# Spreading a gain vector over the partitions with four matmuls instead of a broadcast load, at the head of a hybrid layer

## The chip, the cores and the metric

The kernel runs on one core of one Trainium2 chip. The metric is the device time of one execution in microseconds (us), as the median of several runs; less is better. The engines are named as the profile names them: PE is TensorE (PEld its weight loads), DVE VectorE, ACT ScalarE, POOL GpSimd, SP SyncE, which here only issues transfers (SPq in the rows).

## The reference, cut to what matters

The kernel computes one layer of an encoder for 512 prompt tokens and 64 sample tokens, in fp32, with a width of 2048. Everything starts from a normalised copy of the input:

```python
def rmsnorm(x, g):
    xf = x.astype(jnp.float32)
    xf = xf * lax.rsqrt(jnp.mean(xf * xf, axis=-1, keepdims=True) + RMS_EPS)
    return (xf * g.astype(jnp.float32)).astype(x.dtype)
...
    xn = rmsnorm(x, g_pre)

    def cols(off, width):
        return jnp.einsum('btd,dc->btc', xn, w_in[:, off:off + width])
```

The columns of `w_in` feed three token mixers (pooling, stick-breaking attention, mLSTM) with their gates; their outputs are projected by `w_branch`, merged, projected by `w_out`, normalised and added to x. `g_pre` has 2048 elements, one for each channel, and is the same for every token.

## The kernel before, in words

**Layout and blocks.** Tokens come in five blocks: four of 128 prompt tokens and one of 64 sample tokens. Block m of the input lies in `xt[:, m, :]` with tokens on partitions and the 2048 channels along each partition. So `g_pre`, which varies along the channels, is needed on all 128 partitions: `gpre_b` is a 128x2048 tile.

**The head of the program.** For each block ACT squares and sums the row (`square`, L1150), DVE makes the mean (`mean_square`, L1540), ACT takes the root (`root`, L1155), DVE takes the reciprocal (L1546) and multiplies x by it and by the gain in one instruction (`normalise`, L1549). PE then transposes the block in 16 pieces of 128x128, four to a PSUM bank (`x_block`, L772), and the banks go to `xq`, the even ones by ACT (L1162) and the odd ones by DVE (`x_quads`, L1557). Blocks 0 and 2 to 4 use the PSUM tensor `M`, block 1 uses `pp`. When blocks 0 to 2 are there, the first half of `xq` is split into a high and a low part by ACT (L1169) and DVE (L1566), and PE starts the products (L764) of w_in, also split into `wa_hi` and `wa_lo` (L1137 and L1526).

**The products.** Pairs of column tiles are computed by a Strassen scheme of seven products of 128x288 with quarters of x and w, or sums of them. The sums of x are made once, by DVE (L1570), while the first products run. There are 68 pairs, then the attention and mLSTM heads woven with the branch projections (L916), the output projection (L1099) and the last normalisation.

**What sets the order.** Each engine's program is written out by hand, and semaphores join them. An engine runs its instructions in that order, and what waits holds up all that stands behind it. On DVE the order is: a memset, the casts of `negones` and `negtri` (L1535, L1536), the mean and `normalise` of block 0, those of block 1, the copies of block 0, the mean and `normalise` of block 2, and so on. On ACT: square 0, root 0, square 1, root 1, two copies of block 0, square 2, root 2, two copies of block 1. POOL starts four small loads and then makes the constants `ident`, `ones`, `negones_f` and `negtri_f`, each of which adds one to `consts_ready`. SP issues the loads in the order block 0, `gpre_b`, blocks 1 and 2, half a tile of w_in, block 3, and so on; the load of `gpre_b` reads the vector 128 times, once for each partition.

Of the kernel before, what the change touches and what calls it, by code (L numbers as in the profile page):

```python
# [10 lines left out]
P = 128  # L11
D = 2048
# [163 lines left out]
def hybrid_layer(nc, x_prompt, x_sample, cache_sb_k, cache_sb_v, state_pool, state_ml_c, state_ml_n,  # L176
# [30 lines left out]
    with ctx:  # L207
        start = -(-nc.sbuf_base // 32) * 32

        def sb(name, at, shape, dt=F32):  # L210
            return nc.alloc_sbuf_tensor_at(name, shape, dt, offset=start + at)

        def sem(name):
            return ctx.enter_context(nc.semaphore(name))
# [9 lines left out]
        ones = sb("ones", 41472, [P, P])  # L224
# [5 lines left out]
        R = 43264  # L230
# [24 lines left out]
        gpre_b = sb("gpre_b", R + 110592, [P, D])  # L255
# [2 lines left out]
        negones_f = sb("negones_f", R + 126976, [P, P])  # L258
        negtri_f = sb("negtri_f", R + 127488, [P, P])
        xq = sb("xq", R + 129024, [P, 4, HK, TH])  # L260

        if_w = [sb("if_w0", R + 150784, [P, HK, P]), sb("if_w1", R + 158080, [P, HK, P])]
        if_rows = sb("if_rows", R + 155648, [ROWS, T])
# [82 lines left out]
        def x_bank(m, q):  # L346

            return pp[:, q, :] if m == 1 else M[:, 512 * q:512 * (q + 1)]
# [46 lines left out]


        x_loaded = [sem(f"x_loaded{m}") for m in range(NB)]
        gain_loaded, vectors_loaded, consts_ready = sem("gain_loaded"), sem("vectors_loaded"), sem("consts_ready")
        signs_ready = sem("signs_ready")
        sq_done, ms_ready, root_x_ready, if_loaded = sem("sq_done"), sem("ms_ready"), sem("root_x_ready"), sem("if_loaded")  # L400
        xs_ready, xtr_done, xqa_done, xqd_done = sem("xs_ready"), sem("xtr_done"), sem("xqa_done"), sem("xqd_done")
# [55 lines left out]
        def _(sp):  # L457
# [15 lines left out]
            def x_block(m):  # L473
                if m < NT:
                    sp.dma_start(xt[:, m, :], xp_v[:, m, :]).then_inc(x_loaded[m], 16)
                else:
                    sp.dma_start(xt[0:TS, NT, :], x_sample[0, :, :]).then_inc(x_loaded[NT], 16)
# [5 lines left out]
            def gate_weights():  # L483

                sp.wait_ge(g_stored, 32 * PG)
                for j in range(2):
                    sp.dma_start(if_w[j][:, :, :], w_in_v[:, HK * j:HK * (j + 1), OFF_MI:OFF_MI + P]).then_inc(if_loaded, 16)

            x_block(0)
            sp.dma_start(gpre_b[:, :], g_pre[0, :].partition_broadcast(P)).then_inc(gain_loaded, 16)  # L490
            x_block(1)
            x_block(2)
            sp.dma_start(raw_11(At(0)), w_in_v[:, 0:HK, column_of(0):column_of(0) + P]).then_inc(wa_loaded[0], 16)
# [259 lines left out]
        def _(pe):  # L753
# [23 lines left out]
            def x_block(m):  # L777

                rows = P if m < NT else TS
                pe.wait_ge(xs_ready, m + 1)  # L780
                for q in range(4):
                    if m == 2:
                        pe.wait_ge((xqa_done, xqd_done)[q % 2], q // 2 + 1)
                    elif m == 3:
                        pe.wait_ge((xqa_done, xqd_done)[q % 2], 4 + q // 2 + 1)
                    elif m == 4:
                        pe.wait_ge(xqa_done, 6 + q + 1)
                    transposes([(x_bank(m, q)[:, P * j:P * j + rows],
                                 xt[0:rows, m, (4 * q + j) * P:(4 * q + j + 1) * P]) for j in range(4)]
                               ).then_inc(xtr_done, 1)  # L790

            pe.wait_ge(consts_ready, 4)
            x_block(0)
            x_block(1)
            x_block(2)
# [724 lines left out]
        def _(dve):  # L1520
            steps = Steps(dve, dve_steps)
# [9 lines left out]

            nc.vector.memset(small[:, 0:20], 1.0).then_inc(signs_ready, 1)
            dve.sem_inc(urow_copied, 1)
            dve.wait_ge(consts_ready, 4)
            nc.vector.tensor_copy(negones[:, :], negones_f[:, :]).then_inc(signs_ready, 1)  # L1535
            nc.vector.tensor_copy(negtri[:, :], negtri_f[:, :]).then_inc(signs_ready, 1)  # L1536
# [6 lines left out]
            def normalise(m):  # L1543
                rows = P if m < NT else TS
                dve.wait_ge(root_x_ready, m + 1)
                steps.link(nc.vector.reciprocal(rs_x[:, m:m + 1], rs_x[:, m:m + 1]))  # L1546
                if m == 0:
                    dve.wait_ge(gain_loaded, 16)
                nc.vector.scalar_tensor_tensor(xt[0:rows, m, :], xt[0:rows, m, :], rs_x[0:rows, m:m + 1],  # L1549
                                               gpre_b[0:rows, :], ALU.mult, ALU.mult).then_inc(xs_ready, 1)  # L1550

# [20 lines left out]
            steps.begin(0, NB)  # L1572
            mean_square(0)
            normalise(0)
            mean_square(1)
            normalise(1)
            x_quads(0)
            mean_square(2)
            normalise(2)
            x_quads(1)  # L1580
            x_quads(2)
# [809 lines left out]
```

## Time and profile before

| | before |
|---|---|
| median of 3 runs | 2336.64 us (2335.86 to 2339.87) |
| the profiled execution | 2337.64 us, of which its span 2334.4 us |
| PE busy | 2264.0 us, 97% of the span |
| DVE busy | 1463.8 us, 63% |
| ACT busy | 924.3 us, 40% |
| mean granted PE clock | 0.99 of full |

The span runs from the first to the last instruction of the trace; 3.2 us of the profiled execution lie around it. A row of the timeline has the start in us from the beginning of the span, the duration in us, then engine, line, operation, tiles and shapes; in square brackets stands the idle time ahead of it and what ended that. The page gives groups of instructions with their summed busy time and the mean of one in ns.

### The profile page before, as it was taken

To read this page: it belongs to the slowest core of one execution; us is meant where nothing else is said; L and a number is where in the kernel's file an instruction comes from. 1 tells how busy PE (TensorE), PEld (TensorE's weight loads), DVE (VectorE), ACT (ScalarE), POOL (GpSimd) and SP (SyncE) were. 2 spreads that over 40 slices of the span, in tenths; PEclk is the share of its full clock that TensorE was granted. 3 is DMA by queue.
4 is the path that set the end of the run, shared out by engine and by line. 5 is a ranking of instruction groups with operands and counts; after the bars stand their busy time and mean duration, and the time that the engine had idled before them with its cause. 6 is when DMAs were issued, how large, how long until landed. Compare 5 with 4: busy or idle time off the path is not lost.

```text
span 2334.4 us, 40379 instructions
## 1 busy us (share of the span) xinstructions
PE 2264.0 (97%) x16616; PEld 2226.1 (95%) x16616; DVE 1463.8 (63%) x1641; ACT 924.3 (40%) x1243; POOL 216.6 (9%) x288
## 2 busy tenths in 40 slices
PE   6899999899999999999999999999999999999996
PEld 5899999899999999999999999999898999999996
DVE  7866768556666666667666666664665676653233
ACT  5433433334433344444444444444554333222221
POOL 0000000000100000111000000000343222000000
PEclk9999999999999999999999999999999999999998
DMA  5443434433444444444444444347556556735222
GB/s 154 115 136 92 135 102 126 140 94 109 127 129 115 127 116 117 129 117 125 119 114 129 121 122 122 110 129 234 169 191 209 178 184 188 183 112 187 74 72 98
DMA packets 417517, 312.34 MB, mean 134 GB/s; under 512 B 11213, under 2 KB 378949, under 8 KB 415376
## 3 DMA queue, kind: packets, MB, share of 16 engines
q1 hardware_dynamic: 398512, 248.81, 38.5%
q0 software_dynamic: 18848, 61.25, 7.4%
q8 instruction: 122, 2.00, 0.4%
q14 instruction: 35, 0.29, 0.0%
HBM read 251.11 MB, written 58.90 MB: 133 GB/s over the span
## 4 chain that ended last, share of the span: by engine, by line
PE 89%; DVE 5%; DMA 2%; issue 1%; ACT 1%; POOL 1%; DVEq 0%; SPq 0%; POOLq 0%; ACTq 0%
PE pp L764 64%; PE pp L916 10%; PE pp L1099 8%; PE M L772 1%; PE M L973 1%; PE M L1019 1%; DMA raw_b<-in_w_out_dram 1%; PE M L1036 1%; PE M L953 1%; PE M L875 1%; PE M L943 1%; PE M L764 1%; DMA out_dram<-n_out 1%; DVE xa L1566 0%; PE M L1076 0%
## 5 line engine op out<-in xcount | busy, mean ns | idle before, releaser
L764 PE MATMUL pp<-xa,wa_hi 128*128 128x288 f32 x7584 | 1524.0, 297 | 18.6 <-DVE xa L1566 11.3
L764 PEld LDWEIGHTS pp<-xa,wa_hi 128*128 128x128 f32 x7584 | 1220.3, 188 | 20.6 <-issue 11.2
L764 PE MATMUL pp<-xa,wa_lo 128*128 128x288 f32 x3792 | 1118.8, 295 | 0.0
L764 PEld LDWEIGHTS pp<-xa,wa_lo 128*128 128x128 f32 x3792 | 717.3, 189 | 0.0
L1526 DVE TENSOR_TENSOR wa_lo<-raw_a,wa_hi 128x1024 fp32r<-128x1024 f32 x272 | 338.5, 1247 | 248.2 <-ACT wa_hi L1137 248.1
L1137 ACT ACTIVATE wa_hi<-raw_a 128x1024 fp32r<-128x1024 f32 x272 | 287.2, 1056 | 217.0 <-PE pp L764 204.4
L1526 DVE TENSOR_TENSOR wa_lo<-raw_r,wa_hi 128x1024 fp32r<-128x1024 f32 x134 | 170.8, 1275 | 142.5 <-ACT wa_hi L1137 142.5
L1137 ACT ACTIVATE wa_hi<-raw_r 128x1024 fp32r<-128x1024 f32 x134 | 141.5, 1056 | 132.3 <-PE pp L764 130.2
L916 PE MATMUL pp<-gt_hi,wb_hi 128*128 128x288 f32 x768 | 169.5, 302 | 0.5 <-DVE gz L1883 0.5
L916 PE MATMUL pp<-gt_hi,wb_lo 128*128 128x288 f32 x768 | 164.8, 296 | 0.0
L916 PE MATMUL pp<-gt_lo,wb_hi 128*128 128x288 f32 x768 | 164.6, 296 | 0.0
L2239 POOL DMA_DIRECT2D z_scratch<-zs x60 | 44.0, 733 | 1071.6 <-ACT zs L1285 581.4
L1526 DVE TENSOR_TENSOR wa_lo<-tx_main,wa_hi 128x1024 fp32r<-128x1024 f32 x67 | 82.1, 1226 | 69.5 <-ACT wa_hi L1137 69.5
L916 PEld LDWEIGHTS pp<-gt_hi,wb_hi 128*128 128x128 f32 x768 | 123.6, 190 | 1.1 <-DVE wb_lo L1871 0.7
L1530 DVE TENSOR_TENSOR raw_a<-raw_a 128x1024 f32<-128x1024 f32 x102 | 124.3, 1219 | 0.0
L916 PEld LDWEIGHTS pp<-gt_hi,wb_lo 128*128 128x128 f32 x768 | 123.9, 189 | 0.0
L916 PEld LDWEIGHTS pp<-gt_lo,wb_hi 128*128 128x128 f32 x768 | 123.7, 189 | 0.0
L1871 DVE TENSOR_TENSOR wb_lo<-raw_b,wb_hi 128x1024 fp32r<-128x1024 f32 x80 | 98.3, 1243 | 29.6 <-ACT wb_hi L1372 29.5
L1099 PE MATMUL pp<-m_hi,wb_hi 128*128 128x288 f32 x512 | 111.2, 298 | 1.3 <-DVE wb_lo L1871 1.3
L1372 ACT ACTIVATE wb_hi<-raw_b 128x1024 fp32r<-128x1024 f32 x80 | 83.8, 1052 | 69.1 <-PE pp L1099 30.9
L1099 PE MATMUL pp<-m_hi,wb_lo 128*128 128x288 f32 x512 | 109.9, 296 | 0.0
L1099 PE MATMUL pp<-m_lo,wb_hi 128*128 128x288 f32 x512 | 109.9, 296 | 0.0
(294 smaller groups left out, 2165.8 us busy)
## 6 DMA issues: line engine op xcount, KB each, us to landing
raw_a<-in_w_in_dram SPq DMA_DIRECT2D x204, 512.0 KB, 5.0
raw_r<-in_w_in_dram SPq DMA_DIRECT2D x68, 512.0 KB, 5.0
z_scratch<-zs POOLq DMA_DIRECT2D x60, 576.0 KB, 3.3
raw_b<-in_w_branch_dram SPq DMA_DIRECT2D x48, 512.0 KB, 4.3
raw_b<-in_w_out_dram SPq DMA_DIRECT2D x32, 512.0 KB, 4.4
gz<-z_scratch SPq DMA_DIRECT2D x48, 288.0 KB, 4.4
qkv<-z_scratch SPq DMA_DIRECT2D x23, 288.0 KB, 4.8
gt_hi<-gated_scratch SPq DMA_DIRECT2D x4, 1152.0 KB, 7.3
```

Of the source, the lines that this page charges most:

```text
L764: i = nc.tensor.matmul(out, ws[:, slot, k, :], xa[:, o, part, k, :], start=opens and k == 0 and s == 0, stop=k == HK - 1 and s == 2, skip_ ...
L772: i = nc.tensor.transpose(out, src, ident[0:k, 0:k])
L875: i = nc.tensor.matmul(out, wp[:, k, c * P:(c + 1) * P], pa[:, k, a:a + w], start=k == 0, stop=k == 1)
L916: i = nc.tensor.matmul(out[:, b, :], ws[:, slot, k, :], xs_[:, k, b * TH:(b + 1) * TH], start=k == 0 and q == 0, stop=k == HK - 1 and q == 2)
L943: m = nc.tensor.matmul(M[:, col:col + w], keys, qT[:, q0:q0 + w], start=True, stop=True)
L1099: i = nc.tensor.matmul(out[:, b, :], ws[:, slot, k, :], xs_[:, k0 + k, b * TH:(b + 1) * TH], start=opens and k == 0 and q == 0, stop=close ...
L1137: nc.scalar.activation(wa_hi[:, n.base % RING_A, :, :], src, ACT.Copy).then_inc(wa_hi_ready, 1)
L1372: nc.scalar.activation(wb_hi[:, n.base % RING_B, :, :], raw_b[:, n.base % RAW_B, :, :], ACT.Copy).then_inc(wb_hi_ready, 1)
L1526: nc.vector.tensor_tensor(wa_lo[:, n.base % RING_A, :, :], src, wa_hi[:, n.base % RING_A, :, :].bitcast(F32), ALU.subtract).then_inc(wa_lo ...
L1530: nc.vector.tensor_tensor(out, a, b, ALU.subtract).then_inc(t_ready, 1)
L1871: nc.vector.tensor_tensor(wb_lo[:, n.base % RING_B, :, :], raw_b[:, n.base % RAW_B, :, :], wb_hi[:, n.base % RING_B, :, :].bitcast(F32), A ...
L2239: pool.dma_start(z_v[:, bass.ds(p.times(2).value(-16), 2), :] if p.per else z_v[:, 2 * spill_of(p.base):2 * spill_of(p.base) + 2, :], stag ...
```

## The change

The vector is loaded first of all, as a single row of 8 KB on one partition (`gpre_row`). Four matmuls, each with a contraction over one partition, multiply a column of ones into 512 elements of the row and so leave each element on all 128 partitions of a bank of `M`. DVE copies the four banks to `gpre_b`, ahead of the two casts, and waits for the last copy. The broadcast load of 1 MB and the wait for it in `normalise` are gone. The loads of x blocks 0, 1 and 2 now follow one another.

```diff
+        gpre_row = sb("gpre_row", R + 129024, [1, D])
...
+            sp.dma_start(gpre_row[:, :], g_pre[:, :]).then_inc(gain_loaded, 16)
             x_block(0)
-            sp.dma_start(gpre_b[:, :], g_pre[0, :].partition_broadcast(P)).then_inc(gain_loaded, 16)
             x_block(1)
...
-            pe.wait_ge(consts_ready, 4)
+            def gain():
+
+                pe.wait_ge(consts_ready, 2)
+                pe.wait_ge(gain_loaded, 16)
+                for q in range(4):
+                    nc.tensor.matmul(x_bank(0, q), ones[0:1, :], gpre_row[:, 512 * q:512 * (q + 1)],
+                                     start=True, stop=True).then_inc(gain_spread, 1)
+
+            gain()
             x_block(0)
...
             dve.sem_inc(urow_copied, 1)
+            for q in range(4):
+                dve.wait_ge(gain_spread, q + 1)
+                i = nc.vector.tensor_copy(gpre_b[:, 512 * q:512 * (q + 1)], x_bank(0, q))
+            steps.begin(0, 1)
+            steps.link(i)
+            steps.end(1)
             dve.wait_ge(consts_ready, 4)
...
                 steps.link(nc.vector.reciprocal(rs_x[:, m:m + 1], rs_x[:, m:m + 1]))
-                if m == 0:
-                    dve.wait_ge(gain_loaded, 16)
```

DVE at the start of the program, before the change:

```order
L1532 MEMSET small 128x20
L1535 CAST negones<-negones_f 128x128 [waits consts_ready]
L1536 CAST negtri<-negtri_f 128x128
L1540 TENSOR_SCALAR small<-small 128x1 [waits sq_done]
L1546 RECIPROCAL small<-small 128x1 [waits root_x_ready]
L1549 SCALAR_TENSOR_TENSOR xt<-xt,small,gpre_b 128x2048 [waits gain_loaded,dve_steps]
```

and after it:

```order
L1542 MEMSET small 128x20
L1546 COPY gpre_b<-M 128x512 [waits gain_spread] x4
L1551 CAST negones<-negones_f 128x128 [waits consts_ready,dve_steps]
L1552 CAST negtri<-negtri_f 128x128
L1556 TENSOR_SCALAR small<-small 128x1 [waits sq_done]
L1562 RECIPROCAL small<-small 128x1 [waits root_x_ready]
L1563 SCALAR_TENSOR_TENSOR xt<-xt,small,gpre_b 128x2048 [waits dve_steps]
```

The four copies stand ahead of the casts and of the mean of block 0, so both now come behind the matmuls.

PE at the start of the program, before the change:

```order
L772 MATMUL M<-ident,xt 128x128 [waits xs_ready,consts_ready]
L772 MATMUL M<-ident,xt 128x128 x15
L772 MATMUL pp<-ident,xt 128x128 [waits xs_ready]
L772 MATMUL pp<-ident,xt 128x128 x15
L772 MATMUL M<-ident,xt 128x128 [waits xqa_done,xs_ready]
```

and after it:

```order
L799 MATMUL M<-gpre_row,ones 128x512 [waits gain_loaded,consts_ready]
L799 MATMUL M<-gpre_row,ones 128x512 x3
L774 MATMUL M<-ident,xt 128x128 [waits xs_ready]
L774 MATMUL M<-ident,xt 128x128 x15
L774 MATMUL pp<-ident,xt 128x128 [waits xs_ready]
L774 MATMUL pp<-ident,xt 128x128 x15
```

The four matmuls stand ahead of the transposes of block 0 and are the first that PE does.

## Rows read from the trace of the kernel before

**Rows 1.** The page: span, and busy time of each engine.

```profile
span 2334.4 us, 40379 instructions
...
PE 2264.0 (97%) x16616; PEld 2226.1 (95%) x16616; DVE 1463.8 (63%) x1641; ACT 924.3 (40%) x1243; POOL 216.6 (9%) x288
```

**Rows 2.** Stretches: from:to, length, PE busy (instructions), granted clock, DMA share, GB/s.

```profile
42.30:75.60 33.30, 21.10 (x118) 0.85 0.28 69
...
600.00:1600.00 1000.00, 1000.00 (x7502) 1.00 0.44 122
```

**Rows 3.** The chain that ended last, in order of time: start, us, what.

```profile
1.87 10.41 DMA xt<-in_x_prompt_dram
...
42.27 2.57 DVE xs L1570
...
75.62 4.41 PE pp L764 x20
```

**Rows 4.** The timeline of the head of the program, up to the first transposes.

```profile
0.95 0.41 SPq L475 DMA_DIRECT2D xt<-in_x_prompt_dram  x1
...
5.16 0.20 POOL L2182 MEMSET ones<- 128x128 f32 x1
...
6.04 0.23 DVE L1535 CAST negones<-negones_f 128x128 fp32r<-128x128 f32 x1 [4.95 <-POOL negtri_f L2185]
6.11 1.91 ACT L1150 ACTIVATE junk<-xt 128x2048 f32<-128x2048 f32 x1 [3.67 <-DMA xt<-in_x_prompt_dram]
6.19 0.22 DVE L1536 CAST negtri<-negtri_f 128x128 fp32r<-128x128 f32 x1
...
10.08 2.35 DVE L1549 SCALAR_TENSOR_TENSOR xt<-xt,small,gpre_b 128x2048 f32<-128x2048 f32 x1 [1.34 <-DMA gpre_b<-in_g_pre_dram]
...
12.31 1.91 ACT L1150 ACTIVATE junk<-xt 128x2048 f32<-128x2048 f32 x1 [3.77 <-DMA xt<-in_x_prompt_dram]
...
12.58 3.65 PE L772 MATMUL M<-ident,xt 128*128 128x128 f32 x16 [12.58 <-DVE xt L1549]
```

**Rows 5.** The timeline, from the normalising of block 1 to block 2's transposes.

```profile
14.97 2.35 DVE L1549 SCALAR_TENSOR_TENSOR xt<-xt,small,gpre_b 128x2048 f32<-128x2048 f32 x1
...
15.41 0.60 ACT L1162 ACTIVATE xq<-M 128x512 f32<-128x512 f32 x1 [0.19 <-PE M L772]
15.90 1.90 ACT L1150 ACTIVATE junk<-xt 128x2048 f32<-128x2048 f32 x1
17.23 1.28 DVE L1557 COPY xq<-M 128x512 f32<-128x512 f32 x2
...
18.43 0.14 DVE L1540 TENSOR_SCALAR small<-small 128x1 f32<-128x1 f32 x1
...
19.04 2.35 DVE L1549 SCALAR_TENSOR_TENSOR xt<-xt,small,gpre_b 128x2048 f32<-128x2048 f32 x1
...
21.45 1.97 PE L772 MATMUL M<-ident,xt 128*128 128x128 f32 x16 [0.40 <-DVE xt L1549]
```

**Rows 6.** Groups by line and shape: count, summed busy us, mean ns of one.

```profile
L875 PE MATMUL M<-pa,wp 128*128 128x512 f32 x32 | 15.3, 599 | 0.0
...
L1557 DVE COPY xq<-M 128x512 f32<-128x512 f32 x2 | 1.3, 683 | 0.0
```

**Rows 7.** Stretches, PE alone, columns as in Rows 2.

```profile
12.00:14.00 2.00, 1.42 (x7) 1.00 0.97 400
...
23.40:27.10 3.70, 0.02 (x1) 1.00 1.19 285
...
28.20:31.20 3.00, 3.00 (x15) 0.50 0.75 181
```

**Rows 8.** Transfers by name: count, KB each, us from issue to landing; last, `past_k`'s.

```profile
xt<-in_x_prompt_dram SPq DMA_DIRECT2D x1, 1024.0 KB, 5.1
gpre_b<-in_g_pre_dram SPq DMA_DIRECT2D x1, 1024.0 KB, 8.6
...
DMA to landing us min/median/max: 1.9/2.7/10.4
```

More of the change, by code:

```diff
@@ L397, in hybrid_layer @@
         x_loaded = [sem(f"x_loaded{m}") for m in range(NB)]
-        gain_loaded, vectors_loaded, consts_ready = sem("gain_loaded"), sem("vectors_loaded"), sem("consts_ready")
+        gain_loaded, gain_spread = sem("gain_loaded"), sem("gain_spread")
+        vectors_loaded, consts_ready = sem("vectors_loaded"), sem("consts_ready")
         signs_ready = sem("signs_ready")
```

## The prediction, made before the changed kernel ran

> **What bounds the kernel now.** I read the page's busy times first. PE is busy for 97% of a span of 2334.4 us [rows 1], and from 600 to 1600 us it is busy without a gap [rows 2]. So a change at the head of the program can only move the moment from which PE is the bound. Next I read the chain that ended last. It leaves the load of an x block at 12.28 us (1.87 + 10.41), runs from 42.27 us mostly over DVE, and is PE's from 75.62 us on [rows 3]; between 42.3 and 75.6 us PE is busy for 21.1 of 33.3 us [rows 2]. The chain has no long wait for a transfer in that stretch, so what shifts the first pieces shifts PE's take-over by as much. The question is then by how much the normalising of block 2 (`normalise(2)`, at 19.04 us, [rows 5]) shifts, since the transposes of block 2, the split of x and the first product all hang on it.
>
> Up to there the timeline shows two waits for data [rows 4]. `normalise(0)` starts at 10.08 us, after DVE has waited 1.34 us for the broadcast load, and the square of block 1 starts at 12.31 us, after ACT has waited 3.77 us for the block. The change takes both away. The next limits decide what that is worth.
>
> **The transfers.** Block 0 lands 5.1 us after its issue at 0.95, at 6.05 us. `gpre_b`, of the same 1 MB, lands 8.6 us after its issue, which came 0.47 us later, at 10.0 us [rows 4, 8]. It holds the queue for about 4.0 us. Without it block 1 lands near 12.28 - 4.0 + 0.47 = 8.8 us (an estimate, from these rows). Block 0 goes one issue later: SP spends 0.47 us on the row first, and its square starts at about 6.6 instead of 6.11 and is read out at about 8.7 us.
>
> **When the row is there.** The trace has no load of 8 KB on SP's queue. The smallest there, 64 KB of `past_k`, takes 1.9 us at the least; block 0, with 1 MB, takes 5.1 [rows 8]. So the row lands between 2.9 and 6.05 us. I take the lower end: it is first in an empty queue and smaller than either. Then the row isn't what PE waits for, but `ones`, made by POOL until 5.36 us [rows 4]. PE can start at about 5.4 us; with the upper end it would be 6.1 us, and everything below 0.7 us later.
>
> **The four matmuls.** Their nearest row is the fp32 matmul of 128x128 by 128x512 of the pool mixer: 32 in 15.3 us, 0.478 us each [rows 6]. The mixer runs at full speed; the first transposes don't. 16 transposes take 3.65 us at 12.58 and 1.97 us at 21.45 [rows 4, 5], a factor of 1.85, although the granted clock reads 1.00 in both, for the first by [rows 7]. I take the slow rate, as PE does nothing before: 4 x 0.478 x 1.85 = 3.54 us, so PE is done at 8.94 us. At full speed it would be 1.91 us. The contraction over one partition instead of 128 could make them cheaper; the rows of this kernel don't show it, and I count no gain for it.
>
> The Trainium skill says on this (TensorE: Matmul & The Clock Gate, What's actually happening) that the throttled clock is the default and activity releases it. The slow first transposes agree with it, the granted clock of 1.00 beside them doesn't; the durations decide. The sum above needs only the durations.
>
> **The copies and what stands behind them.** A copy of 128x512 from PSUM takes 0.68 us [rows 6], less than the 0.88 us from matmul to matmul, so three of the four hide behind PE and the last ends at 8.94 + 0.05 + 0.68 = 9.67 us. The casts `negones` and `negtri` come next: from 6.04 to 6.41 us, 0.37 us [rows 4]. They were free before, since DVE waited anyway; now they are on the path. Then the mean, the root on ACT and the reciprocal: from 18.43 to 19.04 us, 0.61 us, for block 2 [rows 5]. `normalise(0)` starts at 9.67 + 0.37 + 0.61 = 10.65 us, **0.57 us later** than now. Its other input, the square of block 0 at 8.7 us, has over 1 us to spare.
>
> **From block 0 to block 2.** `normalise(1)` no longer waits for data: it starts 2.35 + 0.61 = 2.96 us after `normalise(0)`, at 13.6 instead of 14.97 us. The square of block 1 fits: behind root 0, it runs from about 10.4 to 12.5 us. But `normalise(2)` needs the square of block 2, and ACT stands before it with two copies of block 0's transposes. The terms from the rows: `normalise(0)` to the first transpose 2.50 us (10.08 to 12.58), to the second of ACT's copies 2.83 us (to 15.41), to the square 0.49 us (to 15.90) [rows 4, 5]; and from a square to its `normalise` 2.66 us (12.31 to 14.97, block 1) [rows 4, 5]. Sum: 10.65 + 2.50 + 2.83 + 0.49 + 2.66 = 19.13 us, against 19.04. Today the same path would give 18.56, and it is DVE's copies, behind the late `normalise(1)`, that end last (17.23 + 1.28 us, [rows 5]). So the gain of 1.4 us at block 1 is lost at the next wait, ACT for PE's transposes of block 0, which start later. **Net: +0.1 us.**
>
> DVE's extra 2.7 us of copies lie in time that it idled. Blocks 3 and 4 and the first weights land earlier, with slack: nobody waits for them now, and the chain does not name them [rows 3]. Nothing behind 75.62 us is touched.
>
> Against the profiled execution (2337.64 us, span 2334.4) this is a span of 2334.5 and 2337.7 us in all. That execution lies 1.0 above the median, so against the median: 2336.64 + 0.1 = **2336.7 us**.
>
> **The rivals.**
>
> 1. *The clock is up by the transposes of block 0.* The four matmuls keep PE busy for 3.5 us just ahead. For it: activity does raise the rate, since the transposes of block 2 are fast after two slow batches. Against it: PE then idles from 8.9 to 13.2 us, 4.2 us, and after the idle stretch from 23.4 to 27.1 us the granted clock goes down to 0.50 (1.2 of 2.4 GHz) from 28.2 us on [rows 7]. If it holds, ACT's second copy comes after 2.83 / 1.85 = 1.53 us instead of 2.83: -1.3 + 0.1 = -1.2 us, 2335.4 us.
> By the same page of the Trainium skill, TensorE: Matmul & The Clock Gate (What's actually happening), activity lifts the throttle. By that rule the four matmuls would act as the warm-up for the transposes; whether it outlasts the idle stretch no row here shows.
>
> 2. *PE is fast from its first matmul.* For it only the granted clock of 1.00; against it the slow transposes. The copies then bound: 5.4 + 0.5 + 4 x 0.64 + 0.37 + 0.61 = 9.5 us for `normalise(0)`, and with fast transposes 9.5 + 2.50 + 1.53 + 0.49 + 2.66 = 16.7: -2.3 us, 2334.3 us.
>
> 3. *The slow spell of PE moves onto the path.* Today the clock is at half from 28.2 to 31.2 us [rows 7], while PE is ahead of DVE and loses nothing. If it comes later, beside the two products that the chain holds from 34 us, or still holds at the transposes of block 2 (1.97 against 3.65 us), it costs up to 1.7 us: +1.8, 2338.4 us. The transposes of blocks 0 and 1 now follow one another more closely, which speaks against the latter.
>
> 4. *The row lands late, slower than before.* All of the head now hangs on one small load: PE, then DVE, whose mean of block 0 stands behind the copies, then ACT's root, behind which the square of block 1 is queued. Every microsecond by which the row comes after 5.36 us is paid in full. If it took as long as `gpre_b` does (8.6 us [rows 8]), it would land at 9.55 us: +4.3 us, 2340.9 us. It is slower by over 0.2% when it lands after about 9.9 us. Against it: `gpre_b` takes so long since it lies behind block 0 and is 128 times the bytes; the row is ahead of all.
>
> 5. *The change doesn't shorten what it should.* If block 1 landed no earlier than now, `normalise(2)` would still be at 19.1 us, since that wait isn't last any more: the same forecast.
>
> **How the numbers follow.** The 0.2% that a measurement of this kernel can tell from no change is 4.7 us; the three runs shown already spread over 4.0 us. Chances: the forecast with case 5 60%, case 1 13%, case 2 5%, case 3 15%, case 4 4% (of which 2% past 4.7 us); 3% remain for something outside the head, in either direction. That gives faster 0.02, same 0.94, slower 0.04. The range runs from case 2 to case 3 and the spread of the runs above it: 2334.4 to 2339.8 us.
>
> **What would show it.** In the changed trace: the first matmul at about 5.4 us with `ones` as its releaser; four matmuls until about 8.9; `normalise(0)` near 10.65; no wait for the square of block 1; ACT waiting for PE ahead of its second copy; `normalise(2)` near 19.1; PE's unbroken stretch from about 75.7. The step that carries the forecast is the rate of PE in its first four matmuls and 16 transposes: matmuls much shorter than 0.88 us apart or transposes of block 0 in 2 us would make it a gain of 1 to 2 us. A first matmul later than 6.1 us would make it a loss of the same size as the delay. A difference over 4.7 us either way would mean that something outside the head changed, which nothing here foresees.

## The result: slower by 0.13%

| | before | changed |
|---|---|---|
| median | 2336.91 us (2335.65 to 2339.87, 21 runs) | 2339.51 us (2336.94 to 2342.75, 21 runs) |
| ratio to before | | 1.0013, 95% interval 1.0007 to 1.0019 |
| profiled execution, and its span | 2337.64, 2334.4 us | 2341.96, 2340.4 us |
| start of `normalise(2)` | 19.04 us | 22.67 us |
| PE takes the chain over from DVE | 75.62 us | 80.91 us |

The medians are 2.6 us apart, and the interval of the ratio is 1.6 to 4.4 us. I had forecast +0.1 us. The two profiled executions differ by more, 4.3 us, and their spans by 6.0. A second profile of the kernel before (e12 below) has a span of 2336.6 us, so one execution must not be read to the microsecond. What repeats is the head: in every profile of the changed kernel `normalise(2)` starts at 22.66 or 22.67 us, against 19.04 and 19.22 in the two of the kernel before.

The page of the changed kernel, its span and busy times (beside [rows 1]):

```profile
span 2340.4 us, 40399 instructions
...
PE 2273.1 (97%) x16624; PEld 2231.1 (95%) x16624; DVE 1466.5 (63%) x1645; ACT 924.1 (39%) x1243; POOL 216.3 (9%) x288
```

PE has 16624 instructions instead of 16616. The change added four matmuls, and PE did eight.

The timeline of the changed kernel's head, the same instructions as in [rows 4, 5]:

```profile
5.42 7.19 PE L799 MATMUL M<-gpre_row,ones 1*128 1x512 f32 x8 [5.42 <-POOL ones L2196]
...
6.45 1.91 ACT L1160 ACTIVATE junk<-xt 128x2048 f32<-128x2048 f32 x1 [4.01 <-DMA xt<-in_x_prompt_dram]
7.53 0.69 DVE L1546 COPY gpre_b<-M 128x512 f32<-128x512 f32 x1 [6.43 <-PE M L799]
...
12.65 0.69 DVE L1546 COPY gpre_b<-M 128x512 f32<-128x512 f32 x1 [1.02 <-PE M L799]
...
13.37 0.23 DVE L1551 CAST negones<-negones_f 128x128 fp32r<-128x128 f32 x1
...
13.65 0.15 DVE L1556 TENSOR_SCALAR small<-small 128x1 f32<-128x1 f32 x1
13.83 0.20 ACT L1165 ACTIVATE small<-small 128x1 f32<-128x1 f32 x1 [5.38 <-DVE small L1556]
13.94 1.89 ACT L1160 ACTIVATE junk<-xt 128x2048 f32<-128x2048 f32 x1
...
14.26 2.35 DVE L1563 SCALAR_TENSOR_TENSOR xt<-xt,small,gpre_b 128x2048 f32<-128x2048 f32 x1
...
17.15 2.35 DVE L1563 SCALAR_TENSOR_TENSOR xt<-xt,small,gpre_b 128x2048 f32<-128x2048 f32 x1
...
19.53 0.60 ACT L1172 ACTIVATE xq<-M 128x512 f32<-128x512 f32 x1 [1.11 <-PE M L774]
20.02 1.90 ACT L1160 ACTIVATE junk<-xt 128x2048 f32<-128x2048 f32 x1
...
22.67 2.35 DVE L1563 SCALAR_TENSOR_TENSOR xt<-xt,small,gpre_b 128x2048 f32<-128x2048 f32 x1
```

The first row is the new cost: PE spreads the vector from 5.42 to 12.6 us. DVE waits 6.43 us for the first bank and about a microsecond for each of the others (the brackets), and ACT waits 5.38 us for the mean, which stands behind them. The two waits of the kernel before are gone: the square of block 1 (13.94) and `normalise(0)` (14.26) wait for no load. But they now wait for PE, and later than the loads came.

Two pieces of the chain that ended last in the changed kernel (beside [rows 3]):

```profile
5.42 7.21 PE M L799 x8
...
80.91 4.18 PE pp L766 x16
```

The chain has left the load of block 1 and goes through the spreading matmuls. The take-over by PE comes 5.29 us later than at 75.62: 3.63 us of it are there at `normalise(2)`, and 1.66 us come right behind it, at the transposes of block 2:

```profile
16.67 3.68 PE L774 MATMUL M<-ident,xt 128*128 128x128 f32 x16 [4.06 <-DVE xt L1563]
20.14 2.69 PE L774 MATMUL pp<-ident,xt 128*128 128x128 f32 x16
25.08 3.63 PE L774 MATMUL M<-ident,xt 128*128 128x128 f32 x16 [2.25 <-DVE xt L1563]
```

These are PE's transposes of blocks 0, 1 and 2, from the same timeline. The last took 1.97 us before [rows 5], and takes 3.63 here.

### The profile page after: what moved, and what is told of

Its sections match the earlier page's. It is cut to its first block, busy times and chain, and to the rows that moved or that the text cites. A ratio compares the mean times of both kernels' runs of the same rounds, so it can differ in the third digit from the quotient of the medians.

```text
span 2340.4 us, 40399 instructions
## 1 busy us (share of the span) xinstructions
PE 2273.1 (97%) x16624; PEld 2231.1 (95%) x16624; DVE 1466.5 (63%) x1645; ACT 924.1 (39%) x1243; POOL 216.3 (9%) x288
## 4 chain that ended last, share of the span: by engine, by line
PE 91%; DVE 5%; DMA 1%; issue 1%; ACT 1%; POOL 1%; DVEq 0%; SPq 0%; POOLq 0%; ACTq 0%
PE pp L766 64%; PE pp L926 11%; PE pp L1109 8%; PE M L774 2%; PE M L983 1%; PE M L1029 1%; DMA raw_b<-in_w_out_dram 1%; PE M L1046 1%; PE M L963 1%; PE M L885 1%; PE M L953 1%; PE M L766 1%; DVE xa L1580 0%; PE M L1086 0%; DVE XA L1932 0%
```

## The experiments

Three theories stood against one another. **A**: the head pays for the matmuls' duration, twice what I had put down, one for one; the state of PE's clock adds a microsecond or more of its own. **B**: the loads in a row cost something. **C**: the loss is the queueing on DVE and ACT, the mean, the root and the square of block 1 behind the copies. Each run is compared with the kernel before on the same chip. The first column of numbers is from one profile of each run, the others from all its executions.

| run | edit | `normalise(2)` against 19.04 | ratio to before, 95% interval | in us |
|---|---|---|---|---|
| changed | | +3.63 | 1.0013 (1.0007 to 1.0019) | +1.6 to +4.4 |
| e1 | load of 1 MB back in its place | +3.63 | 1.0014 (1.0004 to 1.0023) | +0.9 to +5.4 |
| e2 | matmuls twice | +10.45 | 1.0047 (1.0032 to 1.0062) | +7.5 to +14.5 |
| e3 | mean ahead of the last copy | +2.81 | 1.0014 (1.0005 to 1.0023) | +1.2 to +5.4 |
| e4 | eight fp32r matmuls for the spread | -0.95 | 1.0001 (0.9992 to 1.0010) | -1.9 to +2.3 |
| e5 | changed, gap filled | +2.34 | 1.0022 (1.0013 to 1.0032) | +3.0 to +7.5 |
| e6 | e4 and e3 together | +0.82 | 1.0003 (0.9994 to 1.0012) | -1.4 to +2.8 |
| e7 | e6, gap filled | +0.07 | 1.0010 (1.0001 to 1.0019) | +0.2 to +4.4 |
| e9 | e4, casts ahead of copies | -0.84 | 0.9992 (0.9983 to 1.0001) | -4.0 to +0.2 |
| e10 | e9, gap filled | -1.62 | 0.9994 (0.9985 to 1.0003) | -3.5 to +0.7 |
| e11 | before, gap filled | +0.31 | 1.0005 (0.9995 to 1.0014) | -1.2 to +3.3 |

**e1: the broadcast load back between blocks 0 and 1.**

```diff
             x_block(0)
+            sp.dma_start(gpre_again[:, :], g_pre[0, :].partition_broadcast(P)).then_inc(again_loaded, 16)
             x_block(1)
...
             root(1)
+            act.wait_ge(again_loaded, 16)
...
             normalise(1)
+            dve.wait_ge(again_loaded, 16)
```

ACT and DVE wait for the load ahead of their copies of block 0, because it is written where they will write; neither had to in the trace.

> The changed kernel, with a broadcast load of 1 MB put back between the loads of x blocks 0 and 1, into memory that nobody reads; so the loads stand as before and only the spreading by matmuls is left of the change. Theory A (the size of the spreading): the head waits for the four matmuls, which the trace shows as eight instructions in 7.19 us, and not for x; the square of block 1 starts behind root 0 at 13.9 us either way, so block 1 landing at about 12.4 us instead of 8.8 changes nothing: normalise(2) again at 22.7 us, the time that of the changed kernel (about 2339.5). Rival B (the order of the loads costs or gains something): the time moves by 1 us or more towards or away from 2336.9, with normalise(2) moved as well or a later weight load waited for.

`normalise(2)` stands at 22.67 us, the span at 2340.4 us, as in the changed kernel, and the ratio is nearly the same (the interval is 4.5 us wide). So the half of the change that put the loads in a row moves nothing in the head while the spread is on the path: B falls.

**e2: each spreading matmul twice.**

```diff
                 for q in range(4):
+                    nc.tensor.matmul(x_bank(0, q), ones[0:1, :], gpre_row[:, 512 * q:512 * (q + 1)],
+                                     start=True, stop=True)
                     nc.tensor.matmul(x_bank(0, q), ones[0:1, :], gpre_row[:, 512 * q:512 * (q + 1)],
```

> The changed kernel, with each of the four spreading matmuls done twice. Theory A: the path holds them all: 16 instructions in 14.4 us at the same rate, the last at 19.8 us, normalise(0) at 21.4 instead of 14.26 us, the whole 7 us slower than the changed kernel (about 2346.5). If PE rises to its full rate on the way, 3.6 to 5 us. Rival (the matmuls are not what the head pays for, but the queueing on DVE or the transfers): under 2 us.

Two rows of its timeline, a pair of instructions of the last matmul, and `normalise(0)`:

```profile
17.52 1.91 PE L801 MATMUL M<-gpre_row,ones 1*128 1x512 f32 x2
...
21.09 2.35 DVE L1565 SCALAR_TENSOR_TENSOR xt<-xt,small,gpre_b 128x2048 f32<-128x2048 f32 x1
```

Another 6.83 us of matmuls move `normalise(0)` by 6.83 us (from 14.26) and `normalise(2)` by 6.82. The cost of the spread is paid one for one, as A has it; in the medians, e2 is 6.8 us above e1, on the same chip (2348.22 against 2341.41 us). Four matmuls cost 6.83 us, 1.71 each, through all 14 us: PE doesn't speed up on them.

**e3: the mean ahead of the last copy.** On DVE the casts, the mean and the reciprocal of block 0 now stand ahead of the fourth copy.

```diff
-            for q in range(4):
-                dve.wait_ge(gain_spread, q + 1)
-                i = nc.vector.tensor_copy(gpre_b[:, 512 * q:512 * (q + 1)], x_bank(0, q))
...
             mean_square(0)
-            normalise(0)
+            for q in range(3):
+                dve.wait_ge(gain_spread, q + 1)
+                nc.vector.tensor_copy(gpre_b[:, 512 * q:512 * (q + 1)], x_bank(0, q))
+            dve.wait_ge(root_x_ready, 1)
+            steps.begin(0, NB + 1)
+            steps.link(nc.vector.reciprocal(rs_x[:, 0:1], rs_x[:, 0:1]))
+            dve.wait_ge(gain_spread, 4)
+            steps.link(nc.vector.tensor_copy(gpre_b[:, 1536:2048], x_bank(0, 3)))
...
```

> The changed kernel, with DVE's program in another order: the casts, the mean of block 0 and its reciprocal stand ahead of the last copy instead of behind all four. Theory A: the last copy still ends at 13.35 us, and normalise(0) follows it at once, at 13.4 instead of 14.26 us: 0.85 us faster, the square of block 1 starts at 8.9 instead of 13.9 us. Rival C (the loss is mainly the queueing of the mean, the root and the square of block 1 behind the copies): 2 us or more come back.

```profile
10.31 1.91 ACT L1160 ACTIVATE junk<-xt 128x2048 f32<-128x2048 f32 x1 [1.35 <-DMA xt<-in_x_prompt_dram]
...
12.72 0.69 DVE L1588 COPY gpre_b<-M 128x512 f32<-128x512 f32 x1 [1.02 <-PE M L799]
13.45 2.35 DVE L1589 SCALAR_TENSOR_TENSOR xt<-xt,small,gpre_b 128x2048 f32<-128x2048 f32 x1
```

From e3's timeline: the square of block 1 starts 3.6 us earlier than in the changed kernel, as soon as the block lands at 10.3 us, and that is worth nothing. `normalise(0)` follows the last copy at once, at 13.45 instead of 14.26. The 0.81 us are what A expected; C, which wanted 2 or more, falls. In the time of the runs 0.8 us can't be seen.

**e4: the same spread from fp32r parts.** ACT rounds the row to fp32r, DVE takes the rest, and both are multiplied by a row of ones and added up in the bank. The low part is there to keep what the rounding drops; how near the sum comes to the full vector, no run here measures. The row of ones for it is made by DVE, so PE no longer waits for POOL. The lines that make the parts are left out.

```diff
-                pe.wait_ge(consts_ready, 2)
-                pe.wait_ge(gain_loaded, 16)
+                pe.wait_ge(ones_made, 2)
                 for q in range(4):
-                    nc.tensor.matmul(x_bank(0, q), ones[0:1, :], gpre_row[:, 512 * q:512 * (q + 1)],
-                                     start=True, stop=True).then_inc(gain_spread, 1)
+                    pe.wait_ge(lo_made, q + 1)
+                    nc.tensor.matmul(x_bank(0, q), ones_row[:, :], gain_hi[:, 512 * q:512 * (q + 1)],
+                                     start=True, stop=False)
+                    nc.tensor.matmul(x_bank(0, q), ones_row[:, :], gain_lo[:, 512 * q:512 * (q + 1)],
+                                     start=False, stop=True).then_inc(gain_spread, 1)
```

> The changed kernel, with the row split into a rounded high part (by ACT) and the rest (by DVE), both fp32r, and spread by eight fp32r matmuls that add up in the bank; the column of ones is made by DVE, so PE need not wait for POOL. Theory A: the split costs about 1.3 us before PE can start, the eight take 0.43 us each at half rate, so the last ends at 7.9 to 8.9 us instead of 12.6; normalise(0) at 9.6 to 10.6 instead of 14.26, and 3.7 to 4.7 us come back: about 2335 to 2336. Rival (the cost is not in the matmuls' duration): the time stays at about 2339.5.

From its timeline, the rounding, the second to last and the last matmul, and the three `normalise`:

```profile
2.66 2.19 ACT L1193 ACTIVATE gain_hi<-gpre_row 1x512 fp32r<-1x512 f32 x4 [0.22 <-DMA gpre_row<-in_g_pre_dram]
...
6.92 0.62 PE L804 MATMUL M<-gain_hi,ones_row 1*128 1x512 f32 x1
...
7.35 0.62 PE L806 MATMUL M<-gain_lo,ones_row 1*128 1x512 f32 x1
...
9.62 2.35 DVE L1583 SCALAR_TENSOR_TENSOR xt<-xt,small,gpre_b 128x2048 f32<-128x2048 f32 x1
...
12.94 2.35 DVE L1583 SCALAR_TENSOR_TENSOR xt<-xt,small,gpre_b 128x2048 f32<-128x2048 f32 x1
...
18.09 2.35 DVE L1583 SCALAR_TENSOR_TENSOR xt<-xt,small,gpre_b 128x2048 f32<-128x2048 f32 x1
```

Eight fp32r matmuls take 0.43 us each (6.92 to 7.35), 3.75 us with the last one's end, where four in fp32 take 7.19. The row is there at 2.66 us. `normalise(0)` starts at 9.62 us, 4.64 us ahead of the changed kernel, and the loss is gone: 2337.20 against 2337.76 us before. Of the 4.64 us, 3.44 are the shorter matmuls and 1.20 PE's earlier start (4.22 instead of 5.42 us). With the spread cut to half and begun earlier, and the loads still in a row, the result turns from slower to no difference that the runs can tell.

**e5: the gap filled.** 18 transposes of `ident` into banks that nobody reads, between the spread and block 0's transposes.

```diff
             gain()
+            for j in range(18):
+                nc.tensor.transpose(pp[:, j % 4, 0:P], ident[:, :], ident[:, :])
             x_block(0)
```

> The changed kernel, with 18 transposes of the constant ident between the spreading matmuls and block 0's transposes, which nobody reads; they fill the 4.06 us in which PE idles there. Theory A with the clock as its second term: with PE busy without a gap from 5.4 us, the transposes of block 0 run at the full rate (1.97 us instead of 3.68), ACT's second copy comes 1.2 us earlier, and normalise(2) starts at 21.5 instead of 22.7 us; if block 2's transposes are fast too, another 1.7 us come back: 1.2 to 2.9 us faster than the changed kernel. Rival (the clock doesn't matter for the time): no difference, or up to 1 us slower where the filler is slow and delays block 0.

The transposes of blocks 0, 1 and 2 in its timeline:

```profile
16.67 1.96 PE L774 MATMUL M<-ident,xt 128*128 128x128 f32 x16 [0.61 <-DVE xt L1565]
19.55 1.97 PE L774 MATMUL pp<-ident,xt 128*128 128x128 f32 x16 [0.92 <-DVE xt L1565]
23.78 1.97 PE L774 MATMUL M<-ident,xt 128*128 128x128 f32 x16 [2.26 <-DVE xt L1565]
```

All three run at the full rate, although the gap of 2.26 us ahead of the third is that of the changed kernel. `normalise(2)` comes at 21.38 us and the take-over by PE at 77.96, 2.95 us ahead of the changed kernel. In the profile A's second term is confirmed for blocks 0 and 1. For block 2 it is not, since its rate does not go with the filler alone. Here are its transposes in e3, which has no filler, and in e7, which has one:

```profile
24.26 1.97 PE L774 MATMUL M<-ident,xt 128*128 128x128 f32 x16 [1.80 <-DVE xt L1557]
...
21.52 3.57 PE L779 MATMUL M<-ident,xt 128*128 128x128 f32 x16 [2.05 <-DVE xt L1579]
```

The time of e5's runs is not better: 2340.70 us against 2336.62. The slow spell behind the take-over (below) does not explain it, since PE needs 6.54 us there and 6.56 in the changed kernel.

**e6 and e7: high and low parts in e3's order, without and with filler.**

> The spread by high and low parts of e4 together with the order on DVE of e3: the casts, the mean and the reciprocal of block 0 ahead of the last copy. Theory A: the last copy ends at 8.7 us and the mean's chain, from block 0's square at 8.5 us, is the last to be ready: normalise(0) at 9.2 instead of 9.62 us, normalise(2) at 17.7 (18.1 in e4, 19.04 before): 1.3 us faster than the kernel before in the head, about 2336.4. Rival (a wait for block 1, which lands at 10.3 us, has taken over): normalise(2) stays at 18.1.

> The same with 16 filler transposes of ident in PE's idle time ahead of block 0's transposes. Theory A: transposes of block 0 in 2.0 us instead of 3.3 to 3.7; then block 1's load is what ends last: it lands at 10.3 us, normalise(1) at 12.95, DVE's two copies of block 0 behind it, normalise(2) at 17.2 us, 1.8 us before the kernel before; transposes of block 2 at the full rate. About 2335. Rival (the clock doesn't matter): as e6.

Both missed, and by my own edit. From e6's timeline, the mean and what follows:

```profile
8.61 0.15 DVE L1570 TENSOR_SCALAR small<-small 128x1 f32<-128x1 f32 x1 [1.92 <-ACT junk L1168]
8.68 1.88 DVE L1603 COPY gpre_b<-M 128x512 f32<-128x512 f32 x3
...
11.39 2.35 DVE L1609 SCALAR_TENSOR_TENSOR xt<-xt,small,gpre_b 128x2048 f32<-128x2048 f32 x1
```

DVE waits 1.92 us for the square of block 0 while the banks fill; then it has to copy them. The order that gained 0.8 us where the matmuls came last loses 1.8 us where the square does (11.39 instead of 9.62). In e7 `normalise(0)` comes at 11.53 us, so the filler ends 2.45 us before block 0's transposes, and they take 2.85 us, neither slow nor fast.

**e9 and e10: high and low parts with the casts first, without and with filler.**

```diff
+            dve.wait_ge(consts_ready, 4)
+            nc.vector.tensor_copy(negones[:, :], negones_f[:, :]).then_inc(signs_ready, 1)
+            nc.vector.tensor_copy(negtri[:, :], negtri_f[:, :]).then_inc(signs_ready, 1)
             for q in range(4):
                 dve.wait_ge(gain_spread, q + 1)
```

> The spread by high and low parts of e4, with the two casts ahead of the copies on DVE, the mean behind them. (In e6 the mean stood ahead of copies that were ready before it, and so delayed them.) Theory A: the copies end at 8.7 us, the mean follows at 8.75, normalise(0) at 9.35 instead of 9.62 (e4) and 11.39 (e6), normalise(2) at 17.8 to 18.0 us, 1.1 us earlier than in the kernel before: 2335.5 to 2336.5. Rival (the head is no longer what counts): the time of e4 and e6, with no relation to normalise(0).

> The same with 16 filler transposes of ident in PE's gap between the spread (8.0 us) and block 0's transposes (11.8 us). Theory A: the gap is filled, so blocks 0 to 2 are transposed at the full rate (2.0 us each); the landing of block 1 at 10.3 us then ends last, normalise(2) at 17.2 us, 1.8 us ahead of the kernel before; where no slow spell follows later, 2335. Rival (the filler buys nothing, as it seemed in e7, where it ended 2.45 us before the transposes): 2336 to 2339.

Pieces of the chain that ended last in e10:

```profile
1.78 8.88 DMA xt<-in_x_prompt_dram
...
17.42 2.36 DVE xt L1585
...
74.00 4.95 PE pp L771 x24
```

The load of block 1 ends last again, now at 10.66 us, and PE takes over at 74.00 us, 1.6 us earlier than in the kernel before. The medians are the lowest of all, 2336.01 and 2335.51 us against 2337.52. Both intervals reach 1: they may beat the kernel before by up to 4 us, or not at all. In e9 `normalise(0)` came at 9.72, not at 9.35 as I had expected: the casts waited for POOL's `negtri_f`, the copies behind them began at 6.59, and the last one ended at 9.07.

**e11 and e12: the kernel before, filled, and once more.**

```diff
             pe.wait_ge(consts_ready, 4)
+            for j in range(26):
+                nc.tensor.transpose(pp[:, j % 4, 0:P], ident[:, :], ident[:, :])
             x_block(0)
```

> The kernel before, with 26 filler transposes of ident from 6.0 us on, in PE's idle time ahead of block 0's transposes: the clock by itself, without any change of loads or copies. Theory A: the transposes of blocks 0 to 2 run at the full rate, but normalise(1) waits for block 1's load and DVE's copies follow it, so normalise(2) stays at 19.0 us and the time within 1 us of the kernel before; the clock costs time only where the path goes through PE. Rival (the clock's state decides the result wherever it changes): 1 us or more of difference with normalise(2) unmoved.

> The kernel before once more, for a second look at its clock. Theory A with the second term: block 2's transposes, which start 0.4 us after block 1's, are at the full rate again (1.97 us, where the three looks at the changed head show 3.63, 3.24 and 3.57 behind a gap of 2.0 to 2.3 us). Rival (their rate is chance): slow here too. It also shows whether the 3.2 us that lie around the span in the first look, against 1.6 in all later ones, belong to the kernel or to that execution.

In e11 block 0 is transposed in 1.97 us instead of 3.65, and `normalise(2)` comes 0.31 us later, as `normalise(0)` does by 0.28 with its load: on a path that goes through the load of block 1, a faster PE buys nothing. The transposes of blocks 1 and 2 in e12:

```profile
17.55 1.97 PE L772 MATMUL pp<-ident,xt 128*128 128x128 f32 x16 [1.43 <-DVE xt L1549]
...
21.62 2.84 PE L772 MATMUL M<-ident,xt 128*128 128x128 f32 x16 [2.11 <-DVE xt L1549]
```

and PE's stretch of e12 right behind them (from:to, length, PE busy, granted clock, DMA share, GB/s):

```profile
23.50:27.00 3.50, 0.96 (x5) 0.50 1.19 275
```

Here the rival won half: in the same kernel block 1 is fast this time and block 2 partly slow, and the clock is granted at half (1.2 GHz) already at 23.5 us, where the first profile has 1.00 until 28.2. PE took over at 76.81 us instead of 75.62. So the clock differs from execution to execution of one kernel, and a microsecond or more of any single profile is due to it. The 3.2 us around the span of the first profile are not in e12, which has 1.6. Other executions of the kernel before have more, though: 11 of the 27 beside e9 to e12 have 1.8 to 2.8 us there, and none of the 21 of the changed kernel has over 1.7. Why, no run shows.

**e8: the changed kernel once more.**

> The changed kernel once more, for a second look at the clock. Theory A: spreading again in 7.19 us, normalise(0) at 14.26 and normalise(2) at 22.7 us unless block 0's transposes are fast; whether block 2's transposes take 2.0 or 3.6 us can differ from execution to execution, which would be the second part of the loss and explain why the runs spread over 5.8 us. Rival (they are slow in each execution): 3.6 us again.

`normalise(2)` at 22.66 us; the transposes of block 2 in 3.24 us behind a gap of 2.04. They were slow in all three profiles of this head (3.63, e1 3.57, 3.24) and in one of the two of the kernel before.

## Why the prediction was wrong

**The step that failed is the term "the four matmuls": 3.54 us for what takes 7.19.** I took 0.478 us for an fp32 matmul of 512 columns from 32 rows in 15.3 us [rows 6]. Those 32 are instructions of PE, and the program has 16 such matmuls there (4 groups, 2 halves, 2 steps): each is done in two instructions. The count gave it away: the pool mixer's line has 4 x 2 x 2 x 2 = 32 matmuls in the program, half of them with 512 columns, and 64 in the trace. I didn't compare it with the code. In the changed kernel:

```profile
L799 PE MATMUL M<-gpre_row,ones 1*128 1x512 f32 x8 | 7.2, 1076 | 5.4 <-POOL ones L2196 5.4
```

This row is from the groups by line and shape, between 5 and 13 us. Four matmuls in the program, x8 in the trace. With 8 x 0.478 x 1.85 = 7.07 us the sum would have had `normalise(0)` at 14.2 (measured 14.26), `normalise(2)` at 22.7 (22.67), and a forecast of about 2340.3. The factor of 1.85 for the slow rate held (7.19 / 8 / 0.478 = 1.88).

The range, 2334.4 to 2339.8 us, holds the median of 2339.51 all the same. That is luck: its upper end was case 3 and the spread of the runs, and the term that failed had no bound in it.

The Trainium skill has the cost on another page (FP8 and Floating Point Precision, TensorE Precision Notes): true FP32 takes four passes through the array, where reduced-precision FP32 reads the operand and truncates it. The runs agree: 1.71 us for an fp32 matmul of 512 columns at half rate (e2) and 0.43 for one in fp32r (e4), a ratio of 4.0. Transposes of fp32 data count once each in the trace (x16 for 16), so their rows gave no warning.

**The other steps of the sum.** The row landed by 2.66 us (e4), and PE started at 5.42 with `ones` as its releaser: right. The copy took 0.69 (0.68 forecast), the casts 0.28 from 13.37 to the mean at 13.65 (0.37), the mean to `normalise(0)` 0.61: right. From `normalise(0)` to `normalise(2)` it took 8.41 us (8.48), with ACT waiting 1.11 us for PE ahead of its second copy, as written: right. Block 1 landed at 10.3 us (e3, e4, where ACT waits for it), not at 8.8: it came 2.0 us earlier than before, where I had put down 3.5. That term was too good by nearly half, and harmless, since the square of block 1 stood behind root 0 anyway.

**The rivals.** Case 4 had the mechanism: all of the head hangs on the spread, PE, then DVE's mean behind the copies, then ACT's root and the square, and each microsecond is paid in full. I had hung it on a late load and given it 4%. It came from the size of the matmuls, which I took as known and gave no upper bound. Case 3, the slow spell on the path, came as well in this profile: block 2's transposes cost 1.66 us in the profile, within the 1.7 put down. Behind the take-over there is another spell. In the profile of the changed kernel PE needs 6.56 us (80.91 to 87.47) for what took 5.58 before (75.62 to 81.20). This one is not of the change: e11, with the loads of the kernel before, has it too (75.94 to 82.64, 6.70 us), and e3 and e4, with the changed loads, take 5.58. Case 1 was wrong as it stood, since seven microseconds of spreading didn't lift the rate of block 0's transposes (3.68 us); with the filler of e5 it holds.

**A misreading behind the sum.** I had written that the chain is PE's from 75.62 us on. It isn't: from 439.6 to 458.6 us it leaves PE again, for ACT, DVE and two transfers. From the chain of the kernel before:

```profile
444.48 5.29 DMA gated_scratch<-g_lo
...
450.82 6.11 DMA raw_a<-in_w_in_dram
...
458.60 20.83 PE pp L764 x144
...
579.21 1033.84 PE pp L764 x7752
```

and from that of the changed kernel:

```profile
463.90 21.67 PE pp L766 x144
...
585.36 1033.84 PE pp L766 x7752
```

The shift outlives this wait, as the sum needed: it is 5.29 us at the take-over, 5.30 at the return to PE (463.90 against 458.60) and 6.15 at the last row. But the stretch adds differences of its own. In e12, the kernel before, PE takes over 1.19 us later than in the first profile, and the last row starts 3.22 us later (582.43): the return to PE comes 2.10 us later (460.70), and its next 144 products take 21.94 us instead of 20.83. And of the changed kernel's 21 executions the median span is 2337.9 us, where the profiled one has 2340.4. So the two profiles compare a short execution with a long one, and much of the 6.0 us between their spans is that.

**What stays open.** The head's +3.63 us and the two slow spells behind it (1.66 and 0.98 us in the profile) sum to 6.3 us, the median says +2.6. The interval up to +4.4 us admits the head's part, but not all of the clock's; e1, with the same head, is 3.65 us above the kernel before in the medians. As the clock differs between executions, of both kernels (e12 lost 1.0 us to it against the first profile), that part is probably paid in some and not in others, which was not shown. Nor was a cause for the times of e5 and e7, 2 to 3 us above what their heads say; e10, with a filler too, has no such excess. The clock may be part of it: within the executions of each kernel those with a lower mean granted clock are the longer ones, by about 0.8 us for 0.001 (an estimate from the spans and clocks of all the executions, which scatter widely around it). The mean over its executions is 0.9876 for e7 and 0.9881 for e5, against 0.9888 for the kernel before beside them, which would make 1.0 and 0.5 us of the excess.

## What to carry to other kernels

Before a duration is taken from a group's row, divide its count by the number of such operations in the code: if it isn't one, the row is of a part. For an fp32 matmul on this chip it was two instructions, and four times the time of fp32r. And a large load is not expensive while something else ends last: here the cheap replacement of 1 MB of transfer put 7 us of PE, at its slow rate at the start of the program, ahead of everything.

An order of instructions is right for one ending: putting the mean ahead of the copies gained 0.8 us where PE came last, and lost 1.8 us where the square did.

## What the runs showed of the hardware

PE was busy for 14 us without a break with fp32 matmuls of one row (e2), and each still took 1.71 us at the end. The 26 transposes of 128 rows in e11 took 5.11 us from an idle start, less than 26 at the slow 0.228 us, and the next batch took 1.97 us for 16. In both, the profile's granted clock reads 1.00 over these stretches. The spacing says otherwise. In e4 512 fp32r columns take 0.43 us, 0.84 ns a column. The products, of 288 fp32r columns, take 0.133 us each where the clock reads 1.00 (7502 in 1000 us, [rows 2]), 0.46 ns a column, and 0.235 us, 0.82 ns a column, where it reads 0.50, which is 1.2 GHz. So e4's spread ran at half. A row of the products at half and the row of PE's spreading, both of the changed kernel:

```profile
81.00:85.00 4.00, 4.00 (x17) 0.50 0.97 262
...
5.40:12.60 7.20, 7.18 (x8) 1.00 1.01 339
```

Up to its first change the granted clock in this trace says nothing; the spacing of like instructions does. I had read it so in the prediction, and the runs bear it out.
